# Norm sums taken straight from squares, two norms from one pass, padded copies one step ahead, another slot order and split first loads in a three-block kernel

## The reference

```python
def first_block(x, mem, ...):
    x = layer_norm(DN_ALPHA * x + 0.5 * swiglu_ffn(x, ffn1...), ln1_g, ln1_b)
    y = parallel_mixers(x, ...)          # gated delta rule beside a 31-tap convolution
    x = layer_norm(DN_ALPHA * x + y, ln2_g, ln2_b)
    x = layer_norm(DN_ALPHA * x + memory_cross_attention(x, mem, ...), ln3_g, ln3_b)
    x = layer_norm(DN_ALPHA * x + 0.5 * swiglu_ffn(x, ffn2...), ln4_g, ln4_b)
    return x

def second_block(x, c, ...):
    h = rmsnorm(x, norm_mix_w) * (1.0 + scale1) + shift1      # "b2 in"
    x = x + gate1 * (concatenate([ssd_mixer(h), hgrn2_mixer(h)]) @ w_out)
    h = rmsnorm(x, norm_mlp_w) * (1.0 + scale2) + shift2      # "b2 mlp"
    x = x + gate2 * (square(relu(h @ w_up)) @ w_down)
    return rmsnorm(x, final_norm_w)                           # "b2 final"

def third_block(x, ...):
    h = x
    h = h + even_layer(rms_norm_3(h, e_norm_g), ...)          # "even"
    h = h + odd_layer(rms_norm_3(h, o_norm_g), ...)
    return rms_norm_3(h, final_norm_g)
```

## Time and profile before

| | before |
|---|---|
| median of 3 runs | 4597.37 us (4587.29 to 4598.34) |
| profiled execution | 4600.48 us, its span 4598.6 us |
| PE busy / DVE / ACT | 96% / 57% / 17% of the span |
| mean granted TensorE clock | 0.981 |

### The profile page before, as it was taken

The page is one execution under the profiler, slowest core; times in us unless marked ns, Lnnn a source line. Parts: engine busy times, 40 slices in busy tenths (PEclk is TensorE's granted clock), DMA queues, the critical chain, the costliest instruction groups (busy, mean ns, idle before and its releaser), DMA issues.

```text
span 4598.6 us, 67604 instructions
## 1 busy us (share of the span) xinstructions
PE 4434.1 (96%) x29492; PEld 3356.1 (73%) x29492; DVE 2633.1 (57%) x4616; ACT 803.6 (17%) x1448; POOL 171.0 (4%) x280
## 2 busy tenths in 40 slices
PE   8999999999999999999999999999999998999899
PEld 7888445577887888756655548887888787777767
DVE  5675876354555446546244436565556537888736
ACT  0001012221022000221122110001100005444311
POOL 0000000010000000000000000000000003222100
PEclk9998998999999999999999999999999999999999
DMA  7533452103222222111211122222222210000031
GB/s 249 167 111 65 70 69 55 34 2 74 95 88 74 92 83 85 57 52 37 64 47 38 38 64 92 87 79 83 83 74 83 83 51 11 2 3 2 12 95 52
DMA packets 284071, 310.43 MB, mean 68 GB/s; under 512 B 7168, under 2 KB 277632, under 8 KB 280704
## 3 DMA queue, kind: packets, MB, share of 16 engines
q1 hardware_dynamic: 283776, 306.11, 23.4%
HBM read 303.99 MB, written 2.10 MB: 67 GB/s over the span
## 4 chain that ended last, share of the span: by engine, by line
PE 49%; DVE 5%; ACT 1%; issue 1%; DMA 0%; SPq 0%; DVEq 0%; ACTq 0%
PE ps L397 22%; PE ps L321 11%; PE ps L3182 1%; PE ps L2279 1%; PE ps L366 1%; PE ps L878 1%; PE ps L863 1%; PE ps L894 1%; PE ps L1993 1%; PE ps L1982 1%; PE ps L526 1%; PE ps L3098 0%; PE ps L3482 0%; DVE tmp L3122 0%; DVE w L3334 0%
## 5 line engine op out<-in xcount | busy, mean ns | idle before, releaser
L397 PE MATMUL ps<-main 128*128 128x256 f32 x5440 | 1206.6, 379 | 0.0
L397 PEld LDWEIGHTS ps<-main 128*128 128x128 f32 x5440 | 1032.9, 190 | 141.3
L321 PE MATMUL ps<-main,w 128*128 128x512 f32 (+1 forms) x2528 | 1103.9, 592 | 18.8 <-DMA w<-in_ffn_wg 13.0
L397 PE MATMUL ps<-main,w 128*128 128x256 f32 x4100 | 921.0, 381 | 8.2 <-DMA w<-in_w_in 4.6
L321 PEld LDWEIGHTS ps<-main,w 128*128 128x128 f32 x2528 | 480.1, 193 | 564.0 <-issue 533.8
L397 PEld LDWEIGHTS ps<-main,w 128*128 128x128 f32 x4100 | 782.3, 191 | 120.8 <-issue 5.8
L489 DVE TENSOR_TENSOR main<-main,ps 128x512 f32<-128x512 f32 x175 | 120.4, 688 | 433.5 <-PE ps L397 433.2
L436 ACT COPY main<-ps 128x256 f32<-128x256 f32 x109 | 40.6, 372 | 943.4 <-PE ps L397 943.4
L486 DVE TENSOR_TENSOR main<-main,ps 128x512 f32<-128x512 f32 x109 | 74.8, 687 | 220.6 <-PE ps L397 217.8
L704 DVE SCALAR_TENSOR_TENSOR main<-main,params_sb 128x512 f32<-128x512 f32 x256 | 192.5, 752 | 9.1
L494 DVE TENSOR_TENSOR main<-main,ps 128x512 f32<-128x512 f32 x175 | 120.3, 688 | 82.0 <-PE ps L397 80.0
(11 more groups left out here) (481 smaller groups left out, 4829.4 us busy)
## 6 DMA issues: line engine op xcount, KB each, us to landing
w<-in_w_in SPq DMA_DIRECT2D x58, 1024.0 KB, 6.5
w<-in_e_w_in SPq DMA_DIRECT2D x28, 1024.0 KB, 5.1
main<-in_ada_w SPq DMA_DIRECT2D x24, 1024.0 KB, 5.1
w<-in_ffn_wg SPq DMA_DIRECT2D x22, 1024.0 KB, 6.5
w<-in_ffn_wu SPq DMA_DIRECT2D x22, 1024.0 KB, 6.4
w<-in_o_w_in SPq DMA_DIRECT2D x20, 1024.0 KB, 5.5
w<-in_ffn_wd SPq DMA_DIRECT2D x16, 1024.0 KB, 5.3
w<-in_w_up SPq DMA_DIRECT2D x16, 1024.0 KB, 5.4
```

Of the source, the lines that this page charges most:

```text
L321: i = pe.mm(PS[b][:, 0:n], wv[:, k, f * 128:(f + 1) * 128], g.X(kg + k), start=kg + k == 0, stop=kg + k == g.nk - 1)
L397: t = pe.mm(PS[b][:, 256 * half:256 * half + 256], weight[:, m, :], x(m), start=m == 0, stop=m == n - 1)
```

## The change

- KEPT: 17 fewer in front of the mean of "conv ln", 19 fewer each in ln3 and ln4, 16 fewer in "b2 in"; the 24 of "even" go with that norm's sums.
- Opening: SP loads the first half of the first weights, the first half of X, then the second halves; PE waits for each.
- ln3, ln4, "b2 in" (DIRECT): the first 5, 5 and 3 squares have tiles of their own and PE sums each over the partitions as it comes; DVE adds up only the last ones. In "b2 in" DVE makes the first three squares.
- "b2 final" and "even" get their column sums in one pass: beside the total of squares DVE keeps a total weighted with the squared gain; tiles 6 and 7 go straight to PE, with two columns of weights. rstd of both norms comes from them; H3 is made from X and the product of both gains, and X is normalised later.
- act_mixers and act_ssd: the padded copy of tile q+1 stands in front of the silu of tile q (in the mixers not across the gates of f = 4 and 6).
- Delta rule: kind 2 isn't made in the last chunk; behind it the slots go in the order 1, 0, 2, 3, and "after gdn" waits for the last outputs only.
- The "sgu" loads stand behind block 3's first four weight loads.

```diff
-KEPT = {("mean", "ln3"): 7, ("mean", "ln4"): 7, ("mean", "conv ln"): 21,
-        ("squares", "ln3"): 21, ("squares", "ln4"): 21, ("squares", "b2 in"): 28,
-        ("squares", "b2 mlp"): 4, ("squares", "b2 final"): 10, ("squares", "even"): 24, ("squares", "odd"): 10,
+KEPT = {("mean", "ln3"): 7, ("mean", "ln4"): 7, ("mean", "conv ln"): 4,
+        ("squares", "ln3"): 2, ("squares", "ln4"): 2, ("squares", "b2 in"): 12,
+        ("squares", "b2 mlp"): 4, ("squares", "b2 final"): 10, ("squares", "odd"): 10,
...
+            opening = (g.name, j, kg) == ("ffn1 g", 0, 0)
+            pe.wait_ge(*at("w first" if opening else "w", g.name, j, kg))
...
+                    if opening and k == 4:
+                        pe.wait_ge(*at("w", g.name, j, kg))
...
+            src = src.rearrange("(t p) n -> p t n", p=128)
+            if (g, j, kg) == (FFN["ffn1"][0], 0, 0):
+                sp_opening(sp, to, src)
+                continue
+            sp.e.dma_start(to, src).then_inc(at.add(w_landed[slot], 16, ("w", g.name, j, kg)), 16)
+
+    def sp_opening(sp, w, src):
+        x = io["xT"].rearrange("(t p) n -> p t n", p=128)
+        sp.e.dma_start(w[:, 0:4, :], src[:, 0:4, :]).then_inc(at.add(first_landed[0], 16, ("w first", "ffn1 g", 0, 0)), 16)
+        sp.e.dma_start(X.ap[:, 0:4, :], x[:, 0:4, :]).then_inc(at.add(first_landed[1], 16, ("x0", 0)), 16)
+        sp.e.dma_start(w[:, 4:8, :], src[:, 4:8, :]).then_inc(at.add(w_landed[0], 16, ("w", "ffn1 g", 0, 0)), 16)
+        sp.e.dma_start(X.ap[:, 4:8, :], x[:, 4:8, :]).then_inc(at.add(inputs["x"], 16, ("x0", 4)), 16)
+        for k in (1, 2, 3, 5, 6, 7):
+            at.at["x0", k] = at.at["x0", k // 4 * 4]
...
+    def dve_direct_total(v, name, k):
+        first = DIRECT[name]
+        if k <= first:
+            return
+        for q in (k - 1, k):
+            v.wait_ge(*at("square", name, q))
+        if k > first + 1:
+            v.wait_ge(*at("square total", name, k - 1))
+        v.tt(t512[6], SQUARES[first] if k == first + 1 else t512[6], SQUARES[k], ADD).then_inc(
+            v.inc(sem["dve", "norm"], "square total", name, k), 1)
...
+    def dve_direct_square(v, name, X, ready, k):
+        v.wait_ge(*at(*ready, k))
+        v.tt(SQUARES[k], X(k), X(k), MUL).then_inc(v.inc(sem["dve", "norm"], "square", name, k), 1)
...
+    def act_direct_square(a, name, X, ready, k):
+        a.wait_ge(*at(*ready, k))
+        if k == 7:
+            a.wait_ge(*at("mm", "column", name, 0))
+        a.act(SQUARES[k], X(k), ACT.Square).then_inc(a.inc(sem["act", "norm"], "square", name, k), 1)
...
     def dve_total_squares(v, name, k):
+        if name in DIRECT:
+            return dve_direct_total(v, name, k)
...
-    COLUMNS = ("ln1", "conv ln", "ln2", "sgu", "ln3", "ln4", "b2 in", "b2 mlp", "b2 final", "even", "odd", "final")
+    COLUMNS = ("ln1", "conv ln", "ln2", "sgu", "ln3", "ln4", "b2 in", "b2 mlp", "odd", "final")
+
+    DIRECT = {"ln3": 5, "ln4": 5, "b2 in": 3}
+    SQUARES = [t512[i] for i in (1, 2, 3, 7, 0, 4, 5, 1)]
...
+        direct = DIRECT.get(name, 0)
+        for k in range(direct):
+            pe.wait_ge(*at("square", name, k))
+            for c in range(NT):
+                t = pe.mm(PS[b][:, c:c + 1], SQUARES[k][:, c * 128:(c + 1) * 128], ones[:, 0:1], start=k == c == 0, stop=False)
+            t.then_inc(pe.inc(sem["pe", "norm"], "mm", "column", name, k), 1)
         pe.wait_ge(*at("square total", name, 7))
         for c in range(NT):
-            t = pe.mm(PS[b][:, c:c + 1], t512[6][:, c * 128:(c + 1) * 128], ones[:, 0:1], start=True, stop=True)
+            t = pe.mm(PS[b][:, c:c + 1], t512[6][:, c * 128:(c + 1) * 128], ones[:, 0:1], start=not direct and c == 0,
+                      stop=c == NT - 1)
...
+        for k in range(3 if name == "b2 in" else 0, nt):
+            if name in DIRECT:
+                act_direct_square(a, name, X, ready, k)
+            else:
+                act_square(a, name, X, ready, k, total)
...
+                weights.only((1, 0, 2, 3))
...
         def gates(a, f):
             a.wait_ge(*at("mm", f"gc{f // 2}", f % 2))
             a.act(GC(f), bank(f"gc{f // 2}", f % 2), ACT.Sigmoid).then_inc(a.inc(s, "out", f"gc{f // 2}", f % 2), 1)
+        def padded(a, q):
+            f, i = q // 3, q % 3
+            a.wait_ge(*at("pads", q % 4))
+            if q > 3:
+                a.wait_ge(*at("conv4", q - 4))
...
-                a.wait_ge(*at("pads", q % 4))
-                if q > 3:
-                    a.wait_ge(*at("conv4", q - 4))
-                a.wait_ge(*at("mm", f"qkv{f}", i))
...
                 a.act(Q(q), t512[q % 4], ACT.Silu).then_inc(a.inc(s, "q", q), 1)
...
             if f in (4, 6):
...
         pe.mm(PS[b][:, 8:16], const("gt"), gl[:, c, :], start=True, stop=True).then_inc(
             pe.inc(sem["pe", "gdn"], "mm", "gdn e", c), 1)
...
@@ -1457,7 +1515,8 @@
         yield
         v.wait_ge(*at("out", "gdn e", c))
...
+            pe.wait_ge(*at("out", *before))
+        pe_kept(pe, b, "squares", "b2 final")
+        pe.wait_ge(*at("square total", "b2 final", 5))
+        pe.wait_ge(*at("weighted total", 5))
+        for c in range(NT):
+            for q in range(2):
+                pe.mm(PS[b][:, 2 * c + q:2 * c + q + 1], t512[6 - q][:, c * 128:(c + 1) * 128], ones[:, 0:1],
+                      start=c == q == 0, stop=False)
+        for k in (6, 7):
+            pe.wait_ge(*at("square", "b2 final", k))
+            for c in range(NT):
+                t = pe.mm(PS[b][:, 2 * c:2 * c + 2], t512[1 + k % 3][:, c * 128:(c + 1) * 128], NW[:, 2 * k:2 * k + 2],
+                          start=False, stop=k == 7 and c == NT - 1)
+        t.then_inc(pe.inc(s, "mm", "squares", "b2 final", 7), 1)
+        for q, name in ((1, "even"), (0, "b2 final")):
+            b, before = banks.take("rstd all", name)
+            if before:
+                pe.wait_ge(*at("out", *before))
+            pe.wait_ge(*at("two rstd"))
...
+                          start=True, stop=True)
...
+
...
+        g1, g2 = (params[:, PCOL[n]:PCOL[n] + 8] for n in ("final_norm_w_2", "e_norm_g_3"))
+        w = NW.rearrange("p (k q) -> p k q", q=2)
+        v.tt(NG, g1, g2, MUL).then_inc(v.inc(s, "two gains"), 1)
+        v.fill(w[:, :, 0], 1.0).then_inc(v.inc(s, "two ones"), 1)
+        v.tt(w[:, :, 1], g1, g1, MUL).then_inc(v.inc(s, "two weights"), 1)
...
+    def dve_two_totals(v, k):
+        s = sem["dve", "norm"]
+        v.wait_ge(*at("square", "b2 final", k))
+        v.wait_ge(*at("two weights"))
+        g = NW[:, 2 * k + 1:2 * k + 2]
+        if k:
+            v.wait_ge(*at("weighted total", k - 1))
+            t = v.stt(t512[5], t512[1 + k % 3], g, t512[5], MUL, ADD)
+        else:
+            t = v.ts(t512[5], t512[1], g, None, MUL)
+        t.then_inc(v.inc(s, "weighted total", k), 1)
...
+        s = sem["dve", "norm"]
+        sums, r = (a.rearrange("p (c q) -> p c q", q=2) for a in (bank("squares", "b2 final")[:, 0:8], NR2))
+        v.wait_ge(*at("mm", "squares", "b2 final", 7))
+        v.ts(r[:, :, 0], sums[:, :, 0], 1.0, 1e-6 * D, MUL, ADD).then_inc(v.inc(s, "first sum"), 1)
+        v.wait_ge(*at("first sum"))
+        v.stt(r[:, :, 1], r[:, :, 0], 1e-6, sums[:, :, 1], MUL, ADD).then_inc(v.inc(s, "out", "squares", "b2 final"), 1)
+        v.also("two sums")
+        v.wait_ge(*at("two roots"))
+        v.recip(NR2, NR2).then_inc(v.inc(s, "two rstd"), 1)
+        v.wait_ge(*at("two gains"))
+        v.wait_ge(*at("mm", "rstd all", "even"))
...
+    def dve_first_norm(v):
+        v.wait_ge(*at("mm", "rstd all", "b2 final"))
+        for k in range(8):
+            v.stt(X(k), X(k), par("final_norm_w_2", k), bank("rstd all", "b2 final"), MUL, MUL).then_inc(
+                v.inc(sem["dve", "norm"], "rms", "b2 final", k), 1)
+        v.also("out", "rstd all", "b2 final")
...
-        act_root(a, "b2 final", t512[4])
+        act_two_norms(a)
 
     def dve_block2(v):
         after(v, "ffn2")
-        for k in range(8):
+        for k in range(3):
+            dve_direct_square(v, "b2 in", X, ("ln", "ln4"), k)
+        for k in range(4, 8):
             dve_total_squares(v, "b2 in", k)
...
+        dve_two_weights(v)
...
-                        dve_total_squares(v, "b2 final", f - 2)
+                        dve_two_totals(v, f - 2)
...
-        for f in (6, 7):
-            dve_total_squares(v, "b2 final", f)
-        dve_rms(v, "b2 final", X, ("out", "down1"), X, scale=lambda k: par("final_norm_w_2", k))
+        dve_seven_weights(v, *even_steps()[0])
+        dve_two_norms(v)
...
+        padded(a, 0)
+        for f in range(12):
+            if f < 11:
+                padded(a, f + 1)
...
         s = sem["pe", "even"]
-        input_here("sgu")
-        pe_columns(pe, "even")
         steps = even_steps()
         run(pe_pair(pe, G_even["v"], 0))
         for step in steps[0:3]:
             run(pe_seven(pe, *step))
+        input_here("sgu")
...
-        act_rms(a, "even", X, x3, total=True)
...
```

(60 more changed lines are left out.)

18 lines of the change are left out of this document (9 added, 9 removed).

## The result

| | before | after |
|---|---|---|
| median of the comparison | 4597.1 us (4587.3 to 4598.3) | 4543.4 us (4537.8 to 4557.0) |
| profiled execution, its span | 4600.5, 4598.6 us | 4544.8, 4543.0 us |
| PE / DVE busy | 96% / 57% | 97% / 58% |
| granted TensorE clock | 0.981 | 0.983 |

PEclk, in windows of the profile, is the granted share of TensorE's clock: 1.00 is full, 0.50 half.

A forecast was written before the change was run, and what follows sets the result against it. TensorE (PE, busy 96%) was taken to bound the kernel. Terms 4.5 + 16.0 + 1.0 + 7.5 + 3.0 + 9.5 = 41.5 us, off the 4597.4 us median, gave 4556 us; range 4542 to 4576.

The forecast's parts named there:

- the slot order: First load behind the delta rule: issued sooner, so PE's wait and slow gemm go; gain 7.5 us, at least 4.6.
- Opening: First loads: with halves loaded first, PE starts near 8.5 us; gain 4.5 us, bounds 3.0 and 4.7.
- Conv stage: Convolution stage and "conv ln": earlier copies free the bank, fewer kept matmuls; gain 16 us, bounds 9.8 and 17.
- The lower bound: Convolution stage and "conv ln": if the copies brought nothing, removing 17 kept matmuls would still gain 9.8 us.
- Delta rule: Last chunk's unread transposes and products dropped, 1.0 us; new slot order behind it, 7.5 us.
- rival (b): Copy ring not loosened or DVE binds: "conv ln" gives 9.8, the slot 4.6; 32.4 us gained, 4565 us; chance 0.15.
- Direct sums: ln3, ln4, "b2 in": totals ready sooner but the clock falls; 0, 1.0 and 2.0 us, sum 3.
- Two norms: Block 2's last and block 3's first norm in one pass: gain 9.5 us, bounds 6 and 13.
- rival (a): Clock holds through the columns: direct sums give 9.2, the two norms 13 us; 51 us gained, 4546 us; chance 0.18.
- (c): Slower: with 95 fewer kept matmuls, half clock reaches into the gemms at five places; 4616 us; chance 0.02.
- (d): Parts work but don't add up, DVE or a load being late in gemms behind; 4590 us; chance 0.04.
- The row of ln1: Trace at ln1: gapless 1-column matmuls at clock 0.52, read as showing the clock would fall at ln3, ln4, "b2 in".

The follow-up runs named there:

- a1: The changed kernel run again without any edit, beside the kernel before: 4541.9 us, ratio 0.990.
- b3: Changed kernel with the mixers' padded copies back behind each step, kept matmuls staying at 4: 4563.2 us, ratio 0.9938.
- a3: Changed kernel with only the slot order behind the delta rule undone (slots 0 to 3 in turn): 4558.3 us, ratio 0.9924.
- b1: Changed kernel with the direct column sums of ln3, ln4 and "b2 in" undone, 21, 21 and 28 kept matmuls back: 4554.0 us, ratio 0.992.
- c1: As b1 (direct sums undone in the changed kernel), but with only 2, 2 and 12 kept matmuls: 4552.4 us, ratio 0.9925.
- b2: Changed kernel with 21 instead of 4 kept matmuls ahead of the mean of "conv ln", copies staying ahead: 4553.2 us, ratio 0.9915.

## Why the prediction was right

It forecast 4556 us, 41.5 less; it became 4543.4 us. Sign, range (4542 to 4576) and places were right. Of the 12.6 us that it was too high, the trace gives the reason for 2.2 (43.7 against 41.5, the parts) and the choice of the base most of the rest: three of the first four runs of before, and its profile, were at the upper end of its scatter. That is chance, and so in part is the agreement of the sums: the two norms gave 3.0 us more and the slot order 1.4 less than forecast. From the 4587.8 us beside a1, the forecast's 41.5 us lead to 4546.3, where a1 measured 4541.9.

- *Opening* (4.5): right. PE started 1.0 us sooner than forecast, at 7.48, and its first pair took 1.0 us longer, 16.75. Its slow records stand at a PEclk of 1.00 (7 to 12 us).
- *Conv stage* (16.0): right in sum, 16.1, and in the way: with the 11.3 us that after is ahead by then, the mean starts at 768.4 us, forecast 768.5. The lower bound was wrong: "If the copies brought nothing, 17 kept matmuls would still go: 11.5 us (773.07 to 784.55) less 1.7, 9.8 us." In b3 they bring 4.3. Of the 5.5 us between, 3.4 are the wait that half clock made longer there, and 1.9 the four kept matmuls that stay, which run at half clock (3.57 us to the mean, not 1.7).
- *Delta rule* (1.0 and 7.5): 1.0 and 6.1. The wait for the load and the slow gemm went, as a3 shows, and at that place after wins 7.7 us, the forecast. 1.6 of them are lost ahead of it, at the silu of z, where half clock now lies behind the wait. The sum had no term for this wait, which was 1.32 us long before. The prediction's rival (b) had 4.6 for the slot.
- *Direct sums* (3.0): 3.45, in b1 3.2. From before to after ln3 gave -0.3 (forecast 0), ln4 0.7 (1.0) and "b2 in" 3.0 (2.0). The fall of the clock was foreseen in the right three places.
- *Two norms* (9.5): the term that was mis-sized, 12.5. The prediction took half clock through the columns and a slow gemm. The clock held to the spread: low for 3.4 us from 3109.0 only, columns 3.9 us and not up to 4.9, and the gemm 1.8 us shorter. This is what rival (a) said of this place; of the direct sums it was wrong.
- Rivals (b), (c) and (d) fell: the bank's wait is gone, half clock lasted 10.2 us each in "conv ln", ln3 and ln4, 6.8 in "b2 in" and 3.4 us at the two norms, where (c) needed 17 at each place, and the parts add up to 43.7 us.

The row of ln1 decided between 3 and 9.2 us for the direct sums, and the runs bear it out. The clock fell with and without a long gap: in c1 PE idles 8.70 us and comes back at half clock; at ln3 of after PE has only gaps of 0.47 and 0.58 us ahead of the fall at 1443.3 us, and the clock falls too (0.50 from 1443.5 to 1453 us). (At ln1 of before one gap of 0.65 us stands just ahead of the fall at 419.4 us, 0.50 from 420 to 430 us; the prediction passed over it.)

## What to carry to other kernels

Judge a filling matmul by its place: ahead of a wait that ends later anyway it is free and keeps the clock (c1: 5.8 us at three norms), behind the wait's end it costs its full length (b2: 7.3 us). When an engine's program is in a fixed order, put the copy that frees another engine's bank ahead of its own next step, and look in the ring for all that waits on it (b2 and b3: 8 to 9 us). When a part undone alone costs more than forecast, look first where half clock lay in both traces: it accounts for 3.4 us of b3's 11.8. Where the scatter of runs is wider than an edit, compare when the same instruction starts in two traces, and take the base of a forecast from more than three runs.
